# Two streams for the dense part of a first block, and VectorE for the low halves of the weights

## The reference, cut to what matters

```python
sh, sc, gt = split(silu(c) @ mod_w + mod_b, 3)          # for the latent and for the context
p = (layer_norm(h) * (1 + sc) + sh) @ w_in              # all dense parts of the block
pv, u, fh, g = split_proj(p)                            # pooled 256, rwkv 1408, hgrn 1536, gate 1024
u = w[0] * u[t-1] + w[1] * u[t] + w[2] * u[t+1]         # three taps, per channel
y_r = rwkv_branch(u);  o_h = hgrn_branch(fh)            # scans with state
pool = pool_branch(pv)                                  # centred means of 4 widths, minus u, @ pool_w, * scale
mix = concat([pool, y_r, o_h]) * silu(g)                # latent tokens only
x = layer_norm(ALPHA * h + gt * (mix @ w_out)) * ln_g + ln_b
```

## Time and profile before

| | |
|---|---|
| median of 3 runs | 3291.65 us (3291.47 to 3299.13) |
| the profiled execution | 3303.59 us, span 3301.8 us |
| TensorE, busy | 2618.2 us, 79% of the span |
| VectorE | 1521.2 us, 46% |
| ScalarE | 1007.5 us, 31% |
| GpSimd | 816.2 us, 25% |
| DMA | 227.66 MB, mean 69 GB/s |
| granted TensorE clock | 0.895 of full |

### The profile page before, as it was taken

One profiled execution on the slowest core, in us unless ns is written; L12 is line 12 of the kernel. 1 busy time (PEld: TensorE's weight loads), 2 busy tenths in 40 slices (PEclk: granted clock), 3 DMA queues, 4 the chain that ended last, 5 costly groups with the idle time before them and its releaser, 6 DMA issues. The chain is left out here.

```text
span 3301.8 us, 61311 instructions
## 1 busy us (share of the span) xinstructions
PE 2618.2 (79%) x25258; PEld 2147.4 (65%) x25258; DVE 1521.2 (46%) x2400; ACT 1007.5 (31%) x1524; POOL 816.2 (25%) x479
## 2 busy tenths in 40 slices
PE   2573348858758478896878789999998999889998
PEld 2463327737648357785767668888886744567886
DVE  7778734763353477535354334413422244244142
ACT  2223322232222243334223334412223422255232
POOL 3311113204013022220311132222232200234444
PEclk9795669969779699998989799999999989899999
DMA  4440024400000135320000311211121300223222
GB/s 162 157 169 2 2 84 166 161 1 3 2 2 4 65 142 196 102 90 28 3 2 4 115 45 64 71 57 62 59 70 39 99 8 0 77 76 99 87 96 87
DMA packets 61233, 227.66 MB, mean 69 GB/s; under 512 B 5728, under 2 KB 12128, under 8 KB 59104
## 3 DMA queue, kind: packets, MB, share of 16 engines
q1 hardware_dynamic: 61024, 224.61, 19.5%
HBM read 210.96 MB, written 13.63 MB: 68 GB/s over the span
## 5 line engine op out<-in xcount | busy, mean ns | idle before, releaser
L2482 POOL TENSOR_TENSOR f_wl<-f_stage,f_wh 128x1024 fp32r<-128x1024 f32 (+1 forms) x120 | 316.0, 2634 | 610.7 <-ACT f_wh L2478 610.7
L2478 ACT ACTIVATE f_wh<-f_stage 128x1024 fp32r<-128x1024 f32 (+1 forms) x120 | 137.6, 1146 | 594.5 <-PE f_ps L2571 591.5
L2571 PE MATMUL f_ps<-h_h,f_wh 128*128 128x256 f32 (+1 forms) x704 | 238.5, 341 | 14.2 <-POOL f_wl L2482 12.8
L2732 DVE SCALAR_TENSOR_TENSOR f_xr<-f_ps,cols,f_xr 128x511 f32<-128x511 f32 (+1 forms) x132 | 83.1, 658 | 337.8 <-ACT f_xr L2725 337.3
L2571 PE MATMUL f_ps<-h_h,f_wl 128*128 128x256 f32 (+1 forms) x704 | 237.8, 340 | 0.0
L2571 PE MATMUL f_ps<-h_l,f_wh 128*128 128x256 f32 (+1 forms) x704 | 237.7, 340 | 0.0
L2571 PE MATMUL f_ps<-f_f_ah,f_wl 128*128 128x512 f32 (+1 forms) x528 | 183.8, 355 | 0.0
L2571 PE MATMUL f_ps<-f_f_ah,f_wh 128*128 128x512 f32 (+1 forms) x528 | 183.6, 355 | 0.0
L2571 PE MATMUL f_ps<-f_f_al,f_wh 128*128 128x512 f32 (+1 forms) x528 | 183.5, 354 | 0.0
L2571 PE MATMUL a_in_ps<-h_h,a_in_wh 128*128 128x256 f32 (+1 forms) x400 | 138.1, 349 | 21.9 <-POOL a_in_wl L2482 18.9
L2571 PEld LDWEIGHTS f_ps<-h_h,f_wh 128*128 128x128 f32 x704 | 133.2, 190 | 32.2 <-POOL f_wl L2482 14.0
(11 more groups left out here) (670 smaller groups left out, 6809.4 us busy)
## 6 DMA issues: line engine op xcount, KB each, us to landing
f_stage<-in_ffn_up SPq DMA_DIRECT2D x88, 512.0 KB, 3.5
f_stage<-in_ffn_down SPq DMA_DIRECT2D x32, 704.0 KB, 4.0
p_hgrn_mm_side_w<-in_ada_w SPq DMA_DIRECT2D x12, 1536.0 KB, 6.4
a_in_stage<-in_ab_w SPq DMA_DIRECT2D x25, 512.0 KB, 3.5
u_mm_side_w<-in_ada_w SPq DMA_DIRECT2D x11, 1024.0 KB, 5.0
mod_w<-in_mod_w SPq DMA_DIRECT2D x8, 1024.0 KB, 14.1
a_in_side_w<-in_ada_w SPq DMA_DIRECT2D x8, 1024.0 KB, 7.1
p_hgrn_mm_stage<-in_w_in SPq DMA_DIRECT2D x12, 512.0 KB, 7.0
```

The costliest lines, as they stand in the source:

```text
L2478: self.nc.scalar.activation(self.wh[:, slot, :w], self.stage[:, slot, :w], ACT.Copy).then_inc(self.w_high, 1)
L2482: self.nc.gpsimd.tensor_tensor(self.wl[:, slot, :w], self.stage[:, slot, :w], self.wh[:, slot, :w].bitcast(F32), ALU.subtract).then_inc(se ...
L2571: done = self.nc.tensor.matmul(out[s][:, :tn], w, x[:, k, t0:t0 + tn], start=k == 0 and n == 0, stop=k == job.kt - 1 and n == 2)
L2732: nc.vector.scalar_tensor_tensor(out, b[:, :n - 1], self.tap(part, 0, i), out, ALU.mult, ALU.add).then_inc(self.before_ok[part], 1)
```

## The change

`scan_in` replaces `normed`, the masks' load stage and the `dense` of the hgrn tiles: one stage with the layer norm ahead of a `Row` of nine v and z tiles (both spans) and three q tiles (latent span only). The mean of all 768 tokens is signalled once; centring, squares and variance go tile by tile. Masks, `w_up` and `a_up` are loaded in it. Its Gemv takes two tiles a turn and its loads follow one turn behind.

`gates_in` replaces `clear`, the `dense` of the pooled, gate and u tiles and `pool_branch`: one `Row` of 2 + 8 + 11 tiles; the three first u tiles come last and for the latent span only. VectorE makes the sums of the pooling between the pooled and the gate tiles, TensorE its four products between gate and u. The gate is stored to DRAM at tile 14.

`Row.low_on_dve` makes the low halves on VectorE in these two stages, in w_out and in a_in; there GpSimd has no part in it any more. In c_in, c_heads, ab_out, c_out and the two ffn stages it stays on GpSimd. The Gemv tiles are shared out anew: 24 in scan_in, 22 in gates_in, 8 in w_out, 16 and 12 in a_in, 6 in c_in and 8 in c_out; a third `modulation` stage of the later part stands between c_out and f1. In c_in the store of x is issued after the last Gemv load.

```diff
-    t["mask64"] = buf("mask64", [P, len(M64), C])
-    load(nc, "hgrn_masks", [(t["mask64"][:, :, :], t["dram"]["masks64"])])
...
+    def low_on_dve(self, dve, g, slot, w):
+        dve.wait_ge(self.w_high, g + 1)
+        self.nc.vector.tensor_tensor(self.wl[:, slot, :w], self.stage[:, slot, :w],
+                                     self.wh[:, slot, :w].bitcast(F32), ALU.subtract).then_inc(self.w_low, 1)
...
+            if lows and g + 2 < self.total:
+                self.low_on_dve(dve, g + 2, slot, self.width_at(g + 2))
             if job.side is not None:
                 job.side.sums(self.nc, dve, g - job.side_from, slot)
...
+            if weights and k == 3:
+                weights(0)
...
+def scan_in(nc, t, d, x, mods, hh, hl, p, side, also):
+    over = t["over_d"]
+    with Stage(nc, "p_hgrn") as st:
+        xr, sq, rstd = st.sbuf("xr", [P, 3, T]), st.sbuf("sq", [P, 2, T]), st.sbuf("rstd", [P, T])
+        feed = Feed(nc, st, x, KD, 0, T, rstd, *mods_of(mods, 0, (1, 0)), hh, hl, xr)
+        to_vz = Job(d["w_in"], O_HGRN + NR, 9, KD, hh, hl, SEGS, act=copied(nc, p[:, NR:, :], SEGS), side=side)
+        to_q = Job(d["w_in"], O_HGRN, NR, KD, hh, hl, LAT_ONLY, act=copied(nc, p, LAT_ONLY), side=side)
+        row = Row(nc, st, KD * P, [to_vz, to_q])
+        side.place(st)
+        mean, var = st.banks("mean", 2), st.banks("var", 2)
+        mean_ok, centered, squared, summed, log_ok, rstd_ok, moved = (
+            st.sem(s) for s in ("mean", "centered", "squared", "summed", "log", "rstd", "moved"))
+        job_at = [job for job in row.jobs for _ in range(job.n)]
+        block = st.block()
+        @block.sync
+        def _(sp):
+            for g, job in enumerate(job_at):
+                row.load_one(sp, job, g, g % 2, False)
+                if g == 1:
+                    side.load_vec(sp)
+                    for dst, src in also:
+                        sp.dma_start(dst, src).then_inc(moved, 16)
+                if g >= 1:
+                    side.load(sp, g - 1, (g - 1) % 2)
+            side.load(sp, row.total - 1, (row.total - 1) % 2)
+            sp.wait_ge(moved, 16 * len(also))
+        @block.tensor
+        def _(pe):
+            row.credits(pe)
+            for s, (t0, n) in enumerate(SEGS):
+                for k in range(KD):
+                    done = nc.tensor.matmul(mean[s][:, :n], over[:, :], x[:, k, t0:t0 + n], start=k == 0, stop=k == KD - 1)
+            done.then_inc(mean_ok, 1)
+            for k in range(KD):
+                pe.wait_ge(squared, k + 1)
+                for s, (t0, n) in enumerate(SEGS):
+                    done = nc.tensor.matmul(var[s][:, :n], over[:, :], sq[:, k % 2, t0:t0 + n], start=k == 0, stop=k == KD - 1)
+                done.then_inc(summed, 1)
+            row.products(pe, to_vz, feed.ready)
+            row.products(pe, to_q)
+        @block.scalar
+        def _(act):
+            row.high(act, 0, 0, KD * P)
+            for k in range(KD):
+                act.wait_ge(centered, k + 1)
+                if k >= 2:
+                    act.wait_ge(summed, k - 1)
+                nc.scalar.activation(sq[:, k % 2, :], x[:, k, :], ACT.Square).then_inc(squared, 1)
+            act.wait_ge(summed, KD)
+            for s, (t0, n) in enumerate(SEGS):
+                nc.scalar.activation(rstd[:, t0:t0 + n], var[s][:, :n], ACT.Ln, bias=eps_col(t, 1e-5)).then_inc(log_ok, 1)
+            act.wait_ge(log_ok, 2)
+            nc.scalar.activation(rstd[:, :], rstd[:, :], ACT.Exp, scale=-0.5).then_inc(rstd_ok, 1)
+            feed.on_act(act, range(KD))
+            row.high(act, 1, 1, KD * P)
+            side.silu(nc, act)
+            for job in row.jobs:
+                row.on_act(act, job)
+        @block.vector
+        def _(dve):
+            side.credits(dve)
+            dve.wait_ge(mean_ok, 1)
+            for k in range(KD):
+                for s, (t0, n) in enumerate(SEGS):
+                    ins = nc.vector.tensor_tensor(x[:, k, t0:t0 + n], x[:, k, t0:t0 + n], mean[s][:, :n], ALU.subtract)
+                ins.then_inc(centered, 1)
+            row.low_on_dve(dve, 0, 0, KD * P)
+            dve.wait_ge(rstd_ok, 1)
+            feed.on_dve(dve)
+            row.low_on_dve(dve, 1, 1, KD * P)
+            dve.wait_ge(side.vec_ok, 1)
+            for job in row.jobs:
+                row.on_dve(dve, job, True)
...
+        to_pool = Job(d["w_in"], O_POOL, 2, KD, hh, hl, LAT_ONLY, act=pool_out)
+        to_gate = Job(d["w_in"], O_GATE, KD, KD, hh, hl, LAT_ONLY, act=gate_out, side=mod_side, side_from=2)
+        to_u = [*(taps(base, 2, SEGS) for base in range(3, 11, 2)), taps(0, 3, LAT_ONLY)]
+        row = Row(nc, st, KD * P, [to_pool, to_gate, *to_u])
+        side.place(st)
+        mod_side.place(st, "mod_side", side)
+        job_at = [job for job in row.jobs for _ in range(job.n)]
+        block = st.block()
+        @block.sync
+        def _(sp):
+            for g, job in enumerate(job_at):
+                row.load_one(sp, job, g, g % 2, False)
+                if g == 1:
+                    mod_side.load_vec(sp)
+                    pool_.load(sp)
+                if 2 <= g < 10:
+                    mod_side.load(sp, g - 2, g % 2)
+                if g == 11:
+                    sp.wait_ge(mod_side.used, KD + 2)
+                    side.load_vec(sp)
+                if g >= 11:
+                    side.load(sp, g - 11, (g - 11) % 2)
+                if g == 14:
+                    sp.wait_ge(row.banks_free, 10 + 2)
+                    sp.dma_start(gate_dram, gate[:, :, :]).then_inc(kept, 16)
+            side.load(sp, row.total - 11, (row.total - 11) % 2)
+            sp.wait_ge(kept, 16)
...
+            mod_side.credits(dve)
+            side.credits(dve)
+            for g in range(2):
+                row.low_on_dve(dve, g, g, KD * P)
+            row.on_dve(dve, to_pool, True)
+            dve.wait_ge(pool_.cleared, 1)
+            dve.wait_ge(row.banks_free, 4)
+            pool_.sums(dve)
+            dve.wait_ge(mod_side.vec_ok, 1)
+            row.on_dve(dve, to_gate, True)
+            pool_.scale(dve)
+            dve.wait_ge(side.vec_ok, 1)
+            for job in to_u:
+                row.on_dve(dve, job, True)
...
+            row_at = [job for job in row.jobs for _ in range(job.n)]
+            for g, job in enumerate(row_at):
+                row.load_one(sp, job, g, g % 2, False)
+                if g == 1:
+                    side.load_vec(sp)
+                if g >= 1:
+                    side.load(sp, g - 1, (g - 1) % 2)
+            side.load(sp, row.total - 1, (row.total - 1) % 2)
             sp.dma_start(x_dram, x[:, :, :]).then_inc(kept, 16)
...
+            feed.on_dve(dve, lambda g: row.low_on_dve(dve, g, g, KD * P))
             dve.wait_ge(side.vec_ok, 1)
             for job in (*to_v, to_u[0]):
-                row.on_dve(dve, job)
```

More of the change, by code:

```diff
@@ L3627, in _ @@
             row.on_act(act, to_gate[1])
-        @block.gpsimd
-        def _(pool):
-            for g in range(2):
-                row.low(pool, g, g, KD * P)
-            for job in row.jobs:
-                row.on_pool(pool, job)
         @block.vector
@@ L3953, in build @@
+                gates_in(nc, t, d, hh, hl, p_pool, pooled, gate, gate_dram, u,
+                         Gemv(d["mod_w"], d["vec_1"], mods, 16, 1), Gemv(d["ada_w"], d["vec_2"], mods2, 24, 2))
             hidden.close()
```

232 lines of the change are left out of this document (169 added, 63 removed).

## The result

The changed kernel takes 3274.6 us (median of 6 runs, 3271.8 to 3277.0); the kernel before takes 3295.1 beside it (6 runs, 3286.5 to 3306.3). The ratio is 0.994, interval 0.9922 to 0.9957: faster by 20 us. The forecast was 3265, range 3238 to 3286. The profiled execution took 3272.4 (span 3270.1) where that of before took 3303.6 (span 3301.8), 31.7 less in span.

A forecast was written before the change was run, and what follows sets the result against it. Barrier-separated stages, with TensorE setting the dense pace while fed, bound the kernel. Terms -39.5 - 17 - 2.5 + 20 + 9 + 3 = -27 took the profiled 3303.6 to 3276.6; less 12 between profile and median, 3265 us, range 3238 to 3286.

The forecast's parts named there:

- Rival A: The forecast itself: the load circles close as worked out, 3265 us, 3250 to 3284 by the terms' bounds; chance 0.62.
- -39.5 for scan_in: Opening stage: the next stage's TensorE starts at 199 instead of 238.45, a gain of 39.5 us (35 to 42).
- The circles: Gates and a_in: load(g+1) waits for low(g) through a Gemv load; laps 10.0 and 13.6 us against 5.44 and 8.34.
- B: Gates and a_in: no circle, TensorE keeps its pace, gates -42, a_in -1, 3219 us; chance 0.1.
- C: Low halves on VectorE cost 2.4 us each, as on GpSimd, giving 3292 us; chance 0.11.
- D: Gates and a_in: pauses keep the granted clock low, gate tile 10.9, a_in tile 16.7, 3304 us; chance 0.07.
- -5.3 for -17: gates_in term: stage ends at 630 for 647.42, a gain of 17 us (-9 to -22; without the circle -42).
- Eight u tiles of 8.34 and three of 5.44 need no such lap (their Gemv loads lag by two more tiles): gates_in, behind the gate tiles: u tiles run at TensorE's pace, 66.7 plus 16.3 us, from 535 to 618.
- +24.5 for +20: a_in term: the circle and the store of x ahead of tile 4 cost 20 us (0 to +25).
- "normalise" and "copies and gates": a_in: VectorE's normalise ahead of low(10) adds 3 us, copies and gates ahead of others add 2.
- +7.0 for +9: c_in term: the store of x behind the last Gemv load ends the stage at 2591.5 for 2582.5, +9 us (5 to 12).
- w_out's term: w_out: without GpSimd's subtraction, one VectorE stop of 2.1 us in the opening goes; -2.5 us (-4 to 0).

The follow-up runs named there:

- run 11: Kernel before with scan_in alone (its low halves on VectorE), twelve modulation tiles left out and set to zero: 3253.7 us.
- run 1: Changed kernel with the Gemv loads of tiles 2 to 7 in a_in issued one tile later: 3248.2 us.
- run 2: Changed kernel with the Gemv loads of the gate tiles in gates_in issued one tile later: 3245.6 us.
- run 6: On top of run 2, load 12 ahead of the wait and the vector, Gemv loads of the u tiles one tile later: 3240.1 us.
- run 3: Changed kernel with the c_in store of x issued behind the load of tile 5, ahead of the last two Gemv loads: 3266.2 us.
- run 4: Changed kernel with the low halves of gates_in back on GpSimd, order of loads unchanged: 3254.5 us.
- run 9: Kernel before, unchanged, profiled once more: 3291.2 us, span 3289.4.
- run 10: Changed kernel with the low halves of a_in back on GpSimd, order of loads unchanged: 3248.5 us.
- run 5: On top of run 2, the 2 MB gate store split into four pieces behind the loads of tiles 14 to 17: 3250.0 us.
- run 7: On top of run 1, the 3 MB a_in store of x split into four pieces behind loads 3 to 6: 3243.3 us.
- run 8: Changed kernel with runs 1, 2, 5, 6, 7, c_in store in four pieces, and tile 4's low half amid the pooling's sums: 3207.2 us.
- run 12: As run 8, but with the stores of gates_in and a_in in one piece again: 3202.3 us.

## Why the prediction was right, and where it was off

**The sign and the mechanism.** Rival A holds: -39.5 for scan_in was -40.0 (the stage behind it starts at 198.5 to 201.8 in all twelve profiles that have scan_in), and run 11 gives the part 41 by itself, without twelve Gemv tiles. The circles are there and closed with the laps worked out: 9.5 for 10.0 in the gates, 13.2 for 13.6 in a_in. B falls, since runs 1 and 2 had to take them away to get its pace. C falls with 1.23 us for a low half. D, which would have made it slower, falls as a cost, not as a fact. Two stretches of the gates after, the clock behind POOL's figures:

```profile
441.00:451.00 10.00, 7.29 (x31) 5.37 (x30) 3.51 (x5) 1.54 (x2) 0.00 (x0) 1.00 0.36 128
451.00:461.00 10.00, 6.77 (x17) 5.36 (x18) 3.51 (x5) 1.54 (x2) 0.00 (x0) 0.66 0.31 108
```

The granted clock did fall behind pauses (mean 0.86 over 441 to 491), and the laps stayed at 9.46 to 9.65, because TensorE had time to spare in each. By the rule of the Trainium skill that D drew on (TensorE: Matmul & The Clock Gate, Part 1) the fall was to be expected; that it cost time no row here shows.

**The terms.** gates_in is the one that was mis-sized: -5.3 for -17. Its laps were a little shorter than taken: the low half of tile 10 ends the sixth at 491 - 403 = 88 behind the stage's start, for 93. The step that failed is "Eight u tiles of 8.34 and three of 5.44 need no such lap (their Gemv loads lag by two more tiles)", with the store "under the u loop". From the high half of tile 11 to the rwkv stage it took 112.8 us; run 6, where u tiles do come at 8.34, has 99.8. The lag keeps a circle from closing, but it doesn't keep a weight load from standing behind a Gemv load that waits for VectorE, and it doesn't help load 12, which I had not followed: it stands behind a wait for the last gate Gemv and behind 2 MB. VectorE has 8.2 of work in 8.34, so it caught up nothing once it was late.

a_in was +24.5 for +20. Of this 14 had gathered by the high half of tile 10, which waits for the products of tile 8, for 15, with tile 4 8 late for 6; the high half of tile 8 itself came 24.5 later, of which 10 was gone two tiles on; what was undersized is the low halves queued behind other work of VectorE, 10 for the 5 of "normalise" and "copies and gates". c_in was +7.0 for +9; run 3 takes back 5.5 of it. w_out gave 1.7 for 2.5, c_out and the modulation 2.4 for 3.

On the low half of GpSimd beside VectorE, which w_out's term rested on: run 4 has a sum at 3.22 for 1.47. The Trainium skill (SBUF — State Buffer, Who interferes with whom) names exactly this pair, a VectorE instruction with two inputs in SBUF beside a GpSimd instruction that reads SBUF, and here the trace agrees.

**The sum and its base.** The edited parts give -13 by the traces (-15 against run 9), where -27 was forecast; the medians give -20. The rest is what the same code takes in different executions. That the profile after took 3272.4, close to the 3276.6 of the sum, is luck: terms 14 too hopeful met 19 that the same code gave. That there would be 12 between profile and median on both sides was wrong too: the kernel before had its dip in that profile, and after the change the median lies 2 above the profile. With the edited parts alone, 13 to 15 below the median of 3295, the time would be some 3281, still in the range. In the chances, 0.60, 0.10 and 0.10 make 0.80 for faster and not 0.82, with 0.13 for no change.

The rwkv stretch took 488.9 to 504.8 us over the profiles, and on the whole the longer ones have the lower mean clock. The shortest (run 10) and the longest (run 5):

```profile
604.00:1093.00 489.00, 317.58 (x7952) 272.33 (x7952) 215.78 (x377) 131.56 (x262) 88.37 (x111) 0.81 0.03 11
```

```profile
576.00:1081.00 505.00, 331.96 (x7953) 285.46 (x7954) 215.90 (x377) 131.38 (x262) 88.31 (x111) 0.77 0.04 11
```

VectorE, ScalarE and GpSimd do the same work in both; TensorE is busy 14 us longer. What sets the clock differently from one execution to the next stays open.

## What to carry to other kernels

When an operation moves to another engine, follow SyncE's queue and not only that engine's load: a load that doesn't need the operation can stand behind one that waits for the engine which now makes it. A background load goes behind the next foreground load, one tile later than it could, and that one line was worth 23 and 27 us here. And price each part of a bundled change by itself: its first part alone, less twelve Gemv tiles, beat the whole by 21 us, and with three orders of loads, one low half and one store put right the whole beat both (3202 for 3254).

## What the hardware did that was not expected

- The granted clock of unchanged code differs between executions: 0.50 for some 20 us of attention in one of two profiles of the same kernel (10.3 us), and 0.77 to 0.81 over the rwkv stretch (16 us). Two profiles of different kernels should be compared stage by stage before a difference is put down to an edit.
- Splitting the 3 MB store of a_in into four gave the next load 5 us and took it from the three behind: over tiles 4 to 7 it was 35.2 us for 34.3 (run 7 and run 1). With the other repairs in place it was 35.1 for 37.3 (run 8 and run 12), so this is not settled.
- Time from the issue of 512 KB of weights to its high half: 4.5 us behind 512 KB (437.83 to 442.32), 5.7 behind 1 MB (1246.02 to 1251.69), 13.5 behind 1 MB, two inputs of 256 KB and the 3 MB store (1225.13 to 1238.62).
